# Gates and ups by one 512-column product: high and low half of the operand side by side, and the halves added by VectorE

## The chip, the cores and the metric

One core of a Trainium2 chip runs the whole program. The metric is the device time of one execution in microseconds (us). The kernel before takes 1074.58 us (median of 3 runs, 1074.38 to 1074.78).

## The reference, cut to what matters

Two layers of a context-and-latent block are followed by a second block of two layers (one attention each) whose second half is a convolutional feed-forward network. Only this network is touched by the change. Its width is 2816, the model width 1024, and there are 256 tokens, all in fp32:

```
def conv_ffn(xn, w_gate, conv_w, conv_b, w_up, w_down):
    g = xn @ w_gate
    gp = jnp.pad(g, ((0, 0), (CONV_WIDTH - 1, 0), (0, 0)))
    gc = conv_b + sum(conv_w[j] * gp[:, j:j + S] for j in range(CONV_WIDTH))
    h = jax.nn.gelu(gc, approximate=False) * (xn @ w_up)
    return h @ w_down
h = h + conv_ffn(rms_norm(h, norm_ffn[i]), ...)     # for i in 0, 1
```

## The kernel before

Every fp32 matrix is split into a high part (rounded to the `fp32r` type) and the rest, the low part. A product is then three matmuls in `fp32r`: high weight by high operand, high weight by low operand, low weight by high operand (`products`, lines 435 to 439). The operand's parts are the tiles OPH and OPL, the weight's parts the three buffers `whi` and `wlo`.

Weights arrive as chunks of 1 MB. SP issues one DMA per chunk into one of three `raw` buffers, when the low part of the chunk three before it is made. ACT copies each half of a chunk to `whi` (`split_hi`, line 400), DVE subtracts it to `wlo` (`split_lo`, line 415). A buffer pair is free when the product with the chunk three before it is done. `split_hi(e, n)` stands in the code where ACT is to have split all chunks below number n; so the place of the call sets ACT's order, and `split_lo` does the same for DVE. All engines work in the order of the code.

The network of a layer (`ffn`) goes through its 2816 columns in 11 passes of 256 (two tiles of 128). Pass c has a chunk for the gate, one for the up product and one for the down product. TensorE's order is gate 0 with up 0 (block by block of the operand), the sum of squares of the norm (line 1008), gate 1, up 1, down 0, gate 2, up 2, down 1, and so on; gate c+1 and up c+1 always stand ahead of down c. A gate or an up chunk is two tiles by eight blocks of the operand, 16 products or 48 matmuls of 256 columns. A down chunk is 48 such matmuls in layer 0 (`narrow`) and 24 of 512 columns in layer 1 (`by_token`), which puts 16 transposes ahead of its first chunk.

In a pass, ACT makes the norm's factor (only at the start, `inverse_root`, lines 1015 and 1019); DVE multiplies the gate's bank by it into a padded tile (line 2959); ACT makes the newest tap of the convolution (2927) and DVE adds two more (2965); ACT takes the Gelu (2934); DVE multiplies the up bank by the factor (2977) and by the Gelu (2980); ACT copies the result to its high part (2939) and DVE subtracts that for the low part (2984), the operand of the down product. Gate and up results alternate over four PSUM banks, so each has a second bank while the first is read. The stage ahead of the network, `added`, uses banks 0 and 1 and empties them into X on DVE (line 2592).

Of the kernel before, what the change touches and what calls it, by code (L numbers as in the profile page):

```python
# [24 lines left out]
P = 128  # L25
# [224 lines left out]
def program(nc, known, stream, first, con, gate_b, b_s, w_s, last_gain, out):  # L250

    with ExitStack() as ctx:
# [4 lines left out]
        def sb(name, shape, dt=F32):  # L257
            return ctx.enter_context(nc.sbuf_tensor(name, shape, dt))
# [5 lines left out]
        OPH, OPL = sb("OPH", [P, KD, T], F32R), sb("OPL", [P, KD, T], F32R)  # L264
# [2551 lines left out]
        def ffn(l, wo, op_free, lo, hidden):  # L2816
# [12 lines left out]
            pad = [PROJ[:, 8192 + 516 * i:8192 + 516 * (i + 1)].rearrange("p (a b) -> p a b", b=SEQ + 2)  # L2829
                   for i in range(2)]  # L2830
            g, up, t1, t2 = [], [], [], []
            for c in range(NF):
# [4 lines left out]
                by["gate", c].used, by["up", c].used = g[c].full, up[c].full  # L2837
                by["down", c].used = ("down_added", l, c)

            def two(m):  # L2840
# [1 line left out]

            rr = r.unsqueeze(1).broadcast_to([P, 2, SEQ])

            def wide(e, u, ch):
                for point in due(e, u.empty, ch.lo):
                    e.wait_ge(*point)
                for t in range(2):
                    for k in range(KD):
                        for point in due(e, op_block(k)):  # L2850
                            e.wait_ge(*point)
                        mm = products(u.mem[:, t * SEQ:(t + 1) * SEQ], cols(ch, k, t * P, P), op(k, lo, SEQ), k == 0,
                                      k == KD - 1)
                mm.then_inc(*raises(u.full))
# [39 lines left out]
            def pe(e):  # L2894
                both = [(g[0], by["gate", 0]), (up[0], by["up", 0])]
                for k in range(KD):
                    for u, ch in both:
                        for point in due(e, u.empty, ch.lo[k // 4], op_block(k)):
                            e.wait_ge(*point)
                        for t in range(2):  # L2900
                            mm = products(u.mem[:, t * SEQ:(t + 1) * SEQ], cols(ch, k, t * P, P), op(k, lo, SEQ),
                                          k == 0 and t == 0, k == KD - 1, skip=True)
                        if k == KD - 1:
                            mm.then_inc(*raises(u.full))
                total.add(e)
                for what, c, ch in order[2:]:
                    if what == "gate":
                        wide(e, g[c], ch)
                    elif what == "up":
                        wide(e, up[c], ch)  # L2910
                    elif l == 0:
                        narrow(e, c, ch)
                    else:
                        by_token(e, c, ch)

            def act(e):
                operand.act(e)
                log_exp_table()
                split_hi(e, first.s + 4)
                inverse_root(e, f"ffn{l}", r, total.tot.mem[:, 0:SEQ], 1.0 / D, total.full, total.tot.read["act"])  # L2920
                for c in range(NF):
                    j = 2 * c
                    split_hi(e, by["gate", c].s + (3 if c else 4))
                    for point in due(e, ("gate_scaled", l, c), t1[c].empty):
                        e.wait_ge(*point)
                    for b in range(2):
                        nc.scalar.activation(t1[c].mem[:, b * SEQ:(b + 1) * SEQ],  # L2927
                                                  pad[c % 2][:, b, 2:SEQ + 2], ACT.Identity,
                                                  bias=vec("conv_b", 22 * l + j + b),
                                                  scale=vec("conv_w", 66 * l + 44 + j + b)).then_inc(*raises(("newest_tap", l, c) if b else ("tap_made", l, c)))  # L2930
# [12 lines left out]
                for i in range(1, 4 if l == 0 else 1):  # L2943
                    s.gives.act(e, (2 * i - 2, 2 * i - 1))

            def dve(e):
                operand.dve(e)
# [2 lines left out]
                split_lo(e, first.s + 3)  # L2950
                for c in range(NF):
                    j = 2 * c
                    split_lo(e, by["gate", c].s + (3 if c else 4))
                    for point in due(e, g[c].full, ("factor_made", f"ffn{l}"), ("pads_zeroed", l, c % 2)):
                        e.wait_ge(*point)
                    if c >= 2:
                        for point in due(e, ("newest_tap", l, c - 2), ("conv_done", l, c - 2)):
                            e.wait_ge(*point)
                    nc.vector.tensor_tensor(pad[c % 2][:, :, 2:SEQ + 2], two(g[c].mem), rr, ALU.mult).then_inc(*raises(("gate_scaled", l, c)))  # L2959
                    for point in due(e, ("newest_tap", l, c), ("gate_scaled", l, c)):  # L2960
                        e.wait_ge(*point)
                    for tap in (1, 0):
                        for b in range(2):
                            x = t1[c].mem[:, b * SEQ:(b + 1) * SEQ]
                            ins = nc.vector.scalar_tensor_tensor(x, pad[c % 2][:, b, tap:tap + SEQ],  # L2965
                                                                 vec("conv_w", 66 * l + 22 * tap + j + b), x,
                                                                 ALU.mult, ALU.add)
                            if tap:
                                ins.then_inc(*raises(("older_tap", l, c, b)))
                            else:  # L2970
                                ins.then_inc(*raises(("conv_done", l, c) if b else ("conv_half_done", l, c)))
                        if tap:
                            e.wait_ge(*when(("older_tap", l, c, 1)))
                    split_lo(e, by["up", c].s + 3)
                    for point in due(e, up[c].full, t2[c].empty):
                        e.wait_ge(*point)
                    nc.vector.tensor_tensor(two(t2[c].mem), two(up[c].mem), rr, ALU.mult).then_inc(*raises(up[c].read["dve"]))
                    for point in due(e, ("gelu_made", l, c), up[c].read["dve"]):
# [8 lines left out]
                split_lo(e, by["down", NF - 1].s + 3)  # L2987
                for i, a in enumerate(acc if l == 0 else ()):
                    for point in due(e, given[i]):
                        e.wait_ge(*point)  # L2990
                    x = X[:, 2 * i:2 * i + 2, 0:SEQ]
                    nc.vector.tensor_tensor(x, two(a.mem), x, ALU.add).then_inc(*raises(a.read["dve"]))
                    if i:
                        s.gives.dve(e, (2 * i - 2, 2 * i - 1))

            for c in range(NF):
                g[c].freed[:] = [("gate_scaled", l, c)]
                t1[c].freed[:] = [t2[c].full]
                t2[c].freed[:] = [("h_lo_made", l, c)]

# [5 lines left out]
            s.operand_used = [up[NF - 1].full]  # L3006
            return s


# [806 lines left out]
```

## Time and profile before

| | us |
|---|---|
| median of 3 runs | 1074.58 |
| the profiled execution | 1075.35 |
| its span in the trace | 1072.7 |
| TensorE busy, matmul | 1064.1 (99%) |
| TensorE busy, weight loads | 949.9 (89%) |
| VectorE busy | 721.6 (67%) |
| ScalarE busy | 574.9 (54%) |

In the profile's rows PE is TensorE's matmuls, PEld its weight loads, DVE VectorE, ACT ScalarE, POOL GpSimd. A matmul's duration holds its way through the array, so consecutive matmuls overlap; the distance of their starts tells what one costs. The profile's chain of work that ended last gives 96% of the span to PE, and 76% of it to the three lines of `products`.

### The profile page before, as it was taken

Reading aid. Unit: us, or ns where it says so; the run is one execution under the profiler, and the core shown is the slowest. Engines: PE = TensorE matmul, PEld = TensorE weight load, DVE = VectorE, ACT = ScalarE, POOL = GpSimd, SP = SyncE. Lnnn points to the kernel's source line nnn. Section 1 sums busy time; section 2 is a strip of 40 time slices with the busy share of each in tenths; the row PEclk is TensorE's granted clock in tenths of the full one; section 3 lists DMA queues with packets and bytes.
Section 4 is the critical chain, followed back from the end, with each engine's and each line's share of the span. In section 5 each row is a group of like instructions: output and inputs, shape, how many; then the busy total and the mean of one; then the engine's idle time right before and its main releaser. Section 6 shows DMA issues by size and latency. Waiting matters only on the chain.

```text
span 1072.7 us, 19921 instructions
## 1 busy us (share of the span) xinstructions
PE 1064.1 (99%) x8092; PEld 949.9 (89%) x8092; DVE 721.6 (67%) x1230; ACT 574.9 (54%) x977; POOL 141.2 (13%) x166
## 2 busy tenths in 40 slices
PE   9999999999999999999999999999999999999998
PEld 7887878656898999799999999999998799999997
DVE  5665566387554878778875676666677776766674
ACT  4532676544444567866565554444574555545454
POOL 0000010253200001632531000000023410000000
PEclk9999999999999999999999999999999999999999
DMA  9732121286613442057444364555543334555641
GB/s 382 319 137 66 75 79 40 93 289 213 232 41 119 141 145 80 6 193 236 148 168 158 119 236 161 194 186 170 198 155 103 134 119 153 202 201 177 211 178 39
DMA packets 25386, 168.77 MB, mean 157 GB/s; under 512 B 3280, under 2 KB 3536, under 8 KB 5456
## 3 DMA queue, kind: packets, MB, share of 16 engines
q1 hardware_dynamic: 25152, 167.25, 44.1%
q8 instruction: 64, 1.05, 0.4%
q10 hardware_dynamic: 144, 0.26, 0.1%
q14 instruction: 26, 0.21, 0.1%
HBM read 164.35 MB, written 1.05 MB: 154 GB/s over the span
## 4 chain that ended last, share of the span: by engine, by line
PE 96%; DVE 2%; ACT 2%; issue 0%; DVEq 0%; ACTq 0%
PE bank L437 26%; PE bank L438 25%; PE bank L439 25%; PE bank L1550 2%; PE bank L494 2%; PE bank L1714 2%; PE bank L1704 2%; PE bank L1694 1%; PE bank L1577 1%; PE bank L1568 1%; PE bank L446 1%; PE bank L2363 1%; PE bank L1395 1%; DVE wlo L415 1%; ACT TILE L1753 1%; PE bank L1688 1%
## 5 line engine op out<-in xcount | busy, mean ns | idle before, releaser
L437 PE MATMUL bank<-OPH,whi 128*128 128x256 f32 (+1 forms) x1716 | 519.7, 303 | 0.3
L439 PE MATMUL bank<-OPH,wlo 128*128 128x256 f32 (+1 forms) x1716 | 511.2, 298 | 0.0
L438 PE MATMUL bank<-OPL,whi 128*128 128x256 f32 (+1 forms) x1716 | 511.2, 298 | 0.0
L415 DVE TENSOR_TENSOR wlo<-raw,whi 128x1024 fp32r<-128x1024 f32 (+1 forms) x255 | 304.0, 1234 | 101.4 <-ACT whi L400 101.3
L437 PEld LDWEIGHTS bank<-OPH,whi 128*128 128x128 f32 x1716 | 328.0, 191 | 17.3 <-issue 5.2
L438 PEld LDWEIGHTS bank<-OPL,whi 128*128 128x128 f32 x1716 | 328.2, 191 | 10.0 <-issue 1.2
L439 PEld LDWEIGHTS bank<-OPH,wlo 128*128 128x128 f32 x1716 | 328.0, 191 | 9.8
L400 ACT ACTIVATE whi<-raw 128x1024 fp32r<-128x1024 f32 (+1 forms) x255 | 254.9, 1050 | 74.2 <-PE bank L439 71.9
L437 PE MATMUL bank<-whi,OPH 128*128 128x256 f32 (+2 forms) x272 | 93.8, 345 | 0.2 <-DVE OPL L717 0.2
L438 PE MATMUL bank<-wlo,OPH 128*128 128x256 f32 (+2 forms) x272 | 91.1, 335 | 0.0
L439 PE MATMUL bank<-whi,OPL 128*128 128x256 f32 (+2 forms) x272 | 91.1, 335 | 0.0
L2927 ACT ACTIVATE TILE<-PROJ,FIRST 128x256 f32<-128x256 f32 x44 | 24.1, 594 | 82.7 <-DVE PROJ L2959 82.7
L437 PEld LDWEIGHTS bank<-whi,OPH 128*128 128x128 f32 x272 | 51.5, 189 | 7.4 <-issue 1.8
L1774 POOL TENSOR_TENSOR TILE<-TILE,STAT 128x512 f32<-128x512 f32 (+1 forms) x48 | 43.0, 918 | 112.8 <-DVE STAT L1765 112.8
L2965 DVE SCALAR_TENSOR_TENSOR TILE<-PROJ,FIRST,TILE 128x256 f32<-128x256 f32 x88 | 38.8, 482 | 26.4 <-ACT TILE L2927 25.6
L1243 ACT ACTIVATE PROJ<-bank 128x512 f32<-128x512 f32 x33 | 19.7, 595 | 66.9 <-PE bank L439 66.8
L438 PEld LDWEIGHTS bank<-wlo,OPH 128*128 128x128 f32 x272 | 51.6, 190 | 4.1 <-issue 0.2
L439 PEld LDWEIGHTS bank<-whi,OPL 128*128 128x128 f32 x272 | 51.5, 189 | 3.9
L999 POOL TENSOR_TENSOR TILE<-TILE 128x512 f32<-128x512 f32 x15 | 21.1, 1409 | 254.5 <-ACT TILE L991 253.8
L2939 ACT ACTIVATE OPH<-TILE 128x512 fp32r<-128x512 f32 x22 | 13.9, 632 | 62.2 <-DVE TILE L2980 62.2
L1646 POOL TENSOR_TENSOR TILE<-TILE,STAT 128x128 f32<-128x128 f32 x64 | 36.2, 595 | 68.4 <-DVE STAT L1600 68.4
L1753 ACT ACTIVATE TILE<-bank,STAT 128x512 f32<-128x512 f32 (+1 forms) x48 | 29.1, 611 | 27.0 <-DVE STAT L1742 27.0
(291 smaller groups left out, 1132.6 us busy)
## 6 DMA issues: line engine op xcount, KB each, us to landing
raw<-in_stream SPq DMA_DIRECT2D x143, 1024.0 KB, 4.9
PROJ<-in_stream SPq DMA_DIRECT2D x5, 1024.0 KB, 18.4
raw<-in_stream SPq DMA_DIRECT2D x4, 1056.0 KB, 8.6
PROJ<-PROJ SPq DMA_DIRECT2D x32, 64.0 KB, 3.9
FIRST<-in_first SPq DMA_DIRECT2D x1, 1248.0 KB, 5.9
C<-in_con SPq DMA_DIRECT2D x1, 1157.5 KB, 7.2
FIRST<-in_first SPq DMA_DIRECT2D x1, 1024.0 KB, 8.0
WST<-in_w_s SPq DMA_DIRECT2D x2, 256.0 KB, 7.3
```

What stands on the lines that cost most here:

```text
L400: nc.scalar.activation(c.w[0][:, part], c.raw[:, part], ACT.Copy).then_inc(*raises(c.hi[h]))
L415: nc.vector.tensor_tensor(c.w[1][:, part], c.raw[:, part], c.w[0][:, part].bitcast(F32), ALU.subtract).then_inc(*raises(c.lo[h]))
L437: nc.tensor.matmul(out, w[0], x[0], start=start, stop=False, skip_group_check=skip)
L438: nc.tensor.matmul(out, w[0], x[1], start=False, stop=False, skip_group_check=skip)
L439: return nc.tensor.matmul(out, w[1], x[0], start=False, stop=stop, skip_group_check=skip)
L494: mm = nc.tensor.matmul(row.mem[32 * j:32 * j + 32, 256 * n:256 * (n + 1)], COND[:, 2 * k:2 * k + 32], c.raw[:, k * 256:(k + 1) * 256], st ...
L1550: mm = nc.tensor.matmul(self.S[p][r].mem[:, at:at + n], q[:, b * P:(b + 1) * P], k[:, 0:n], start=i == 0 and b == 0, stop=i == len(pairs_) ...
L1646: nc.gpsimd.tensor_tensor(x, x, STAT[:, p, 1, i:i + 1].broadcast_to([P, n]), ALU.mult).then_inc(*raises(("p_normed", self.name, p, r) if b ...
L1753: nc.scalar.activation(self.E[j][r].mem[:, 0:n], self.S[j][r].mem[:, 0:n], ACT.Exp, bias=STAT[:, j % 8, 0, r:r + 1], accum_out=STAT[:, j % ...
L1774: nc.gpsimd.tensor_tensor(x, x, STAT[:, j % 8, 1, r:r + 1].broadcast_to([P, n]), ALU.mult).then_inc(*raises(("p_normed", self.name, j, r)))
L2927: nc.scalar.activation(t1[c].mem[:, b * SEQ:(b + 1) * SEQ], pad[c % 2][:, b, 2:SEQ + 2], ACT.Identity, bias=vec("conv_b", 22 * l + j + b), ...
L2965: ins = nc.vector.scalar_tensor_tensor(x, pad[c % 2][:, b, tap:tap + SEQ], vec("conv_w", 66 * l + 22 * tap + j + b), x, ALU.mult, ALU.add)
```

## The change

OPH and OPL become the two halves of one tile OPS, side by side for each block. For gates and ups a product is now two matmuls: high weight by both halves of the operand at once (512 columns, a whole bank), then low weight by the high half (256 columns, added to the bank's first half). Each of the two tiles of a chunk so fills a bank of its own: gates always use banks 2 and 3, ups banks 0 and 1. ACT copies the second halves of both banks to a tile `part`, DVE adds the first halves to it, and only then comes the multiplication by the norm's factor, now from SBUF. Banks are free when that addition is done.

```
+        def products_apart(bank, w, k, lo, start, stop):
+            both = bank[:].rearrange("p (a b) -> p a b", b=SEQ)
+            nc.tensor.matmul(both, w[0], OPS[:, k, :, lo:lo + SEQ], start=start, stop=False, skip_group_check=True)
+            return nc.tensor.matmul(bank[:, 0:SEQ], w[1], OPH[:, k, lo:lo + SEQ], start=False, stop=stop,
+                                    skip_group_check=True)
...
-                g.append(GBANK.take("pe", ("dve",)))
-                up.append(GBANK.take("pe", ("dve",)))
+                g.append([b.take("pe", ("dve",)) for b in banks[2:4]])
+                up.append([b.take("pe", ("dve",)) for b in banks[0:2]])
...
+            def copy_halves(e, what, c, us, both):
+                for point in due(e, us[0].full, us[1].full, ("halves_summed", l, c - 1, what) if c else None):
+                    e.wait_ge(*point)
+                nc.scalar.activation(part[what], both[:, :, SEQ:2 * SEQ], ACT.Copy).then_inc(
+                    *raises(("low_copied", l, c, what)))
+
+            def add_halves(e, what, c, out, both):
+                for point in due(e, ("low_copied", l, c, what), t2[0].empty if c == 0 and what == "up" else None):
+                    e.wait_ge(*point)
+                nc.vector.tensor_tensor(out, both[:, :, 0:SEQ], part[what], ALU.add).then_inc(
+                    *raises(("halves_summed", l, c, what)))
...
             def pe(e):
                 both = [(g[0], by["gate", 0]), (up[0], by["up", 0])]
                 for k in range(KD):
-                    for u, ch in both:
-                        for point in due(e, u.empty, ch.lo[k // 4], op_block(k)):
+                    for us, ch in both:
+                        for point in due(e, [u.empty for u in us], ch.lo[k // 4], op_block(k)):
                             e.wait_ge(*point)
...
             def act(e):
                 operand.act(e)
                 log_exp_table()
+                split_hi(e, first.s + 3)
+                copy_halves(e, "gate", 0, g[0], g_both)
+                copy_halves(e, "up", 0, up[0], up_both)
+                inverse_root(e, f"ffn{l}", r, total.tot.mem[:, 0:SEQ], 1.0 / D, total.full, total.tot.read["act"])
                 split_hi(e, first.s + 4)
-                inverse_root(e, f"ffn{l}", r, total.tot.mem[:, 0:SEQ], 1.0 / D, total.full, total.tot.read["act"])
                 for c in range(NF):
                     split_hi(e, by["gate", c].s + (3 if c else 4))
+                    if c:
+                        copy_halves(e, "gate", c, g[c], g_both)
...
                     nc.scalar.activation(t1[c].mem[:], t1[c].mem[:], ACT.Gelu).then_inc(*raises(("gelu_made", l, c)))
+                    if c:
+                        copy_halves(e, "up", c, up[c], up_both)
+                    split_hi(e, by["up", c].s + 4)
...
                     nc.scalar.activation(HH[c % 2], two(t2[c].mem), ACT.Copy).then_inc(*raises(("h_hi_made", l, c)))
-                    split_hi(e, by["up", c].s + 4)
-                log_exp_table()
-                split_hi(e, by["down", NF - 1].s + 3)
+                if l:
+                    log_exp_table()
+                split_hi(e, by["down", NF - 1].s + 2.5)
                 for i in range(1, 4 if l == 0 else 1):
                     s.gives.act(e, (2 * i - 2, 2 * i - 1))
+                    if i == 1:
+                        split_hi(e, by["down", NF - 1].s + 3)
+                log_exp_table()
...
             def dve(e):
...
+                    add_halves(e, "gate", c, padded, g_both)
+                    if c == 0:
+                        add_halves(e, "up", 0, two(t2[0].mem), up_both)
+                        split_lo(e, first.s + 4)
...
-                    nc.vector.tensor_tensor(pad[c % 2][:, :, 2:SEQ + 2], two(g[c].mem), rr, ALU.mult).then_inc(*raises(("gate_scaled", l, c)))
+                    nc.vector.tensor_tensor(padded, padded, rr, ALU.mult).then_inc(*raises(("gate_scaled", l, c)))
...
-                    nc.vector.tensor_tensor(two(t2[c].mem), two(up[c].mem), rr, ALU.mult).then_inc(*raises(up[c].read["dve"]))
+                    if c:
+                        add_halves(e, "up", c, two(t2[c].mem), up_both)
...
+                    nc.vector.tensor_tensor(two(t2[c].mem), two(t2[c].mem), rr, ALU.mult).then_inc(*tick("dve"))
```

The change also writes the first pass of a layer in another order. These are ACT's rows of that pass in layer 0, from the split of the second and third weights to the high part of the down product's operand; `whi<-raw` x2 is the split of one chunk, KDUP the norm's factor. Before:

```order
L400 ACTIVATE whi<-raw 128x1024 x4
L1015 ACTIVATE KDUP<-bank,SINGLES 128x256
L1019 ACTIVATE KDUP<-KDUP 128x256
L2927 ACTIVATE TILE<-PROJ,FIRST 128x256 x2
L2934 ACT_TABLE_LOAD
L2934 ACTIVATE TILE<-TILE 128x512
L2939 ACTIVATE OPH<-TILE 128x2x256
L400 ACTIVATE whi<-raw 128x1024 x2
```

And now, in the same place on ACT:

```order
L401 ACTIVATE whi<-raw 128x1024 x2
L2869 ACTIVATE PROJ<-bank 128x512 x2
L1023 ACTIVATE KDUP<-bank,SINGLES 128x256
L1027 ACTIVATE KDUP<-KDUP 128x256
L401 ACTIVATE whi<-raw 128x1024 x2
L2953 ACTIVATE TILE<-PROJ,FIRST 128x256 x2
L2960 ACT_TABLE_LOAD
L2960 ACTIVATE TILE<-TILE 128x512
L401 ACTIVATE whi<-raw 128x1024 x2
L2968 ACTIVATE OPS<-TILE 128x2x256
```

The two copies and the factor moved ahead of the split of up 1, and the split of down 0 moved ahead of the high part. On DVE the rows of the same pass, from the split of gate 1 to that of down 0, were these:

```order
L415 TENSOR_TENSOR wlo<-raw,whi 128x1024 x4
L2959 TENSOR_TENSOR PROJ<-bank,KDUP 128x2x256
L2965 SCALAR_TENSOR_TENSOR TILE<-PROJ,FIRST,TILE 128x256 x4
L2977 TENSOR_TENSOR TILE<-bank,KDUP 128x512
L2980 TENSOR_TENSOR TILE<-TILE 128x512
L2984 TENSOR_TENSOR OPL<-TILE,OPH 128x2x256
L415 TENSOR_TENSOR wlo<-raw,whi 128x1024 x2
```

And they are now, on DVE:

```order
L416 TENSOR_TENSOR wlo<-raw,whi 128x1024 x2
L2875 TENSOR_TENSOR PROJ<-bank,PROJ 128x2x256
L2875 TENSOR_TENSOR TILE<-bank,PROJ 128x512
L416 TENSOR_TENSOR wlo<-raw,whi 128x1024 x2
L2999 TENSOR_TENSOR PROJ<-PROJ,KDUP 128x2x256
L3005 SCALAR_TENSOR_TENSOR TILE<-PROJ,FIRST,TILE 128x256 x4
L3021 TENSOR_TENSOR TILE<-TILE,KDUP 128x512
L3025 TENSOR_TENSOR TILE<-TILE 128x512
L3029 TENSOR_TENSOR OPS<-TILE,OPS 128x2x256
L416 TENSOR_TENSOR wlo<-raw,whi 128x1024 x2
```

Two additions came in between the split of gate 1 and that of up 1; the rest keeps its order.

## Rows read from the trace of the kernel before

**Rows 1.** The page: span, TensorE's granted clock in 40 slices (tenths)

```profile
span 1072.7 us, 19921 instructions
...
PEclk9999999999999999999999999999999999999999
```

**Rows 2.** PE's timeline in an up chunk: start us, duration us, engine, line, operation

```profile
660.14 0.28 PE L437 MATMUL bank<-OPH,whi 128*128 128x256 f32 x1
...
660.50 0.28 PE L437 MATMUL bank<-OPH,whi 128*128 128x256 f32 x1
```

**Rows 3.** PE's timeline where products have 512 columns

```profile
64.55 0.39 PE L437 MATMUL bank<-OPH,whi 128*128 128x512 f32 x1
...
65.23 0.39 PE L437 MATMUL bank<-OPH,whi 128*128 128x512 f32 x1
```

**Rows 4.** PE's timeline where 400 columns stand ahead of 512

```profile
20.08 0.34 PE L439 MATMUL bank<-whi,OPL 128*128 128x400 f32 x1
20.26 0.39 PE L437 MATMUL bank<-OPH,whi 128*128 128x512 f32 x1
20.49 0.40 PE L438 MATMUL bank<-OPL,whi 128*128 128x512 f32 x1
```

**Rows 5.** Busy time by engine, passes 3 to 10 of layer 0

```profile
640.00:760.00 120.00, 120.00 (x1003) 120.00 (x1002) 80.00 (x98) 56.93 (x70) 0.00 (x0) 1.00 0.53 185
```

**Rows 6.** DVE's timeline: the gate of pass 3, idle time and releaser in brackets

```profile
640.18 0.69 DVE L2959 TENSOR_TENSOR PROJ<-bank,KDUP 128x512 f32<-128x512 f32 x1 [2.13 <-PE bank L439]
```

**Rows 7.** PE's timeline, first pass of layer 0: gate 1 begins, up 1 ends, down 0

```profile
599.01 0.47 PE L437 MATMUL bank<-OPH,whi 128*128 128x256 f32 x1
...
610.60 0.28 PE L439 MATMUL bank<-OPH,wlo 128*128 128x256 f32 x1
611.00 0.36 PE L437 MATMUL bank<-OPH,whi 128*128 128x256 f32 x1
```

**Rows 8.** ACT's timeline, first pass of layer 0

```profile
598.31 2.01 ACT L400 ACTIVATE whi<-raw 128x1024 fp32r<-128x1024 f32 x2 [6.81 <-PE bank L439]
600.22 0.45 ACT L1015 ACTIVATE KDUP<-bank,SINGLES 128x256 f32<-128x256 f32 x1
600.71 0.42 ACT L1019 ACTIVATE KDUP<-KDUP 128x256 f32<-128x256 f32 x1
...
605.45 0.63 ACT L2934 ACTIVATE TILE<-TILE 128x512 f32<-128x512 f32 x1 [0.56 <-DVE TILE L2965]
606.85 0.63 ACT L2939 ACTIVATE OPH<-TILE 128x512 fp32r<-128x512 f32 x1 [0.77 <-DVE TILE L2980]
607.39 1.99 ACT L400 ACTIVATE whi<-raw 128x1024 fp32r<-128x1024 f32 x2
```

**Rows 9.** DVE's timeline, end of the stage before and first pass of layer 0

```profile
587.45 0.69 DVE L2592 TENSOR_TENSOR FIRST<-bank,FIRST 128x512 f32<-128x512 f32 x1 [0.59 <-PE bank L439]
...
599.50 2.36 DVE L415 TENSOR_TENSOR wlo<-raw,whi 128x1024 fp32r<-128x1024 f32 x2 [4.81 <-ACT whi L400]
601.78 0.69 DVE L2959 TENSOR_TENSOR PROJ<-bank,KDUP 128x512 f32<-128x512 f32 x1
603.62 1.80 DVE L2965 SCALAR_TENSOR_TENSOR TILE<-PROJ,FIRST,TILE 128x256 f32<-128x256 f32 x4 [1.16 <-ACT TILE L2927]
...
607.51 0.69 DVE L2984 TENSOR_TENSOR OPL<-TILE,OPH 128x512 fp32r<-128x512 f32 x1 [0.70 <-ACT OPH L2939]
608.53 2.36 DVE L415 TENSOR_TENSOR wlo<-raw,whi 128x1024 fp32r<-128x1024 f32 x2 [0.33 <-ACT whi L400]
```

**Rows 10.** ACT's timeline: a copy of 512 columns out of a bank

```profile
504.56 0.60 ACT L1243 ACTIVATE PROJ<-bank 128x512 f32<-128x512 f32 x1 [1.96 <-PE bank L439]
```

**Rows 11.** The chain that ended last: the transposes ahead of down 0, layer 1

```profile
902.07 1.75 PE bank L2880 x16
```

**Rows 12.** DMA issues: weight chunks, size, median us to landing

```profile
raw<-in_stream SPq DMA_DIRECT2D x143, 1024.0 KB, 4.9
```

**Rows 13.** Who waited for whom, PE: total us, times, longest

```profile
PE bank L446 <- DVE ONES L767: 1.1, 1, 1.1
```

More of the change, by code:

```diff
@@ L2831, in ffn @@
             g, up, t1, t2 = [], [], [], []
+            g_both, up_both = twin[1], twin[0]
+            part = {what: PROJ[:, at:at + 512].rearrange("p (a b) -> p a b", b=SEQ)
+                    for what, at in (("gate", 9224), ("up", 9736))}
             for c in range(NF):
-                g.append(GBANK.take("pe", ("dve",)))
-                up.append(GBANK.take("pe", ("dve",)))
+                g.append([b.take("pe", ("dve",)) for b in banks[2:4]])
+                up.append([b.take("pe", ("dve",)) for b in banks[0:2]])
                 t1.append(tile.take("act", ("dve",)))
                 t2.append(tile.take("dve", ("act", "dve")))
-                by["gate", c].used, by["up", c].used = g[c].full, up[c].full
+                by["gate", c].used, by["up", c].used = g[c][1].full, up[c][1].full
                 by["down", c].used = ("down_added", l, c)
@@ L2843, in ffn, with wide @@
             rr = r.unsqueeze(1).broadcast_to([P, 2, SEQ])
-            def wide(e, u, ch):
-                for point in due(e, u.empty, ch.lo):
+            def wide(e, us, ch):
+                for point in due(e, ch.lo):
                     e.wait_ge(*point)
-                for t in range(2):
+                for t, u in enumerate(us):
+                    for point in due(e, u.empty):
+                        e.wait_ge(*point)
                     for k in range(KD):
[L2850 to L2854, printed above, removed]
+                        mm = products_apart(u.mem, cols(ch, k, t * P, P), k, lo, k == 0, k == KD - 1)
+                    mm.then_inc(*raises(u.full))
+            def copy_halves(e, what, c, us, both):
[5 more added lines that the diff above has]
+                for point in due(e, ("low_copied", l, c, what), t2[0].empty if c == 0 and what == "up" else None):
+                    e.wait_ge(*point)
+                nc.vector.tensor_tensor(out, both[:, :, 0:SEQ], part[what], ALU.add).then_inc(
+                    *raises(("halves_summed", l, c, what)))
             def narrow(e, c, ch):
@@ L2896, in pe @@
                 for k in range(KD):
-                    for u, ch in both:
-                        for point in due(e, u.empty, ch.lo[k // 4], op_block(k)):
+                    for us, ch in both:
+                        for point in due(e, [u.empty for u in us], ch.lo[k // 4], op_block(k)):
                             e.wait_ge(*point)
[L2900 to L2904, printed above, removed]
+                        for t, u in enumerate(us):
+                            mm = products_apart(u.mem, cols(ch, k, t * P, P), k, lo, k == 0, k == KD - 1)
+                            if k == KD - 1:
+                                mm.then_inc(*raises(u.full))
                 total.add(e)
@@ L2952, in dve @@
                     j = 2 * c
-                    split_lo(e, by["gate", c].s + (3 if c else 4))
-                    for point in due(e, g[c].full, ("factor_made", f"ffn{l}"), ("pads_zeroed", l, c % 2)):
+                    padded = pad[c % 2][:, :, 2:SEQ + 2]
+                    if c:
+                        split_lo(e, by["gate", c].s + 3)
+                    for point in due(e, ("pads_zeroed", l, c % 2)):
                         e.wait_ge(*point)
@@ L2958, in dve @@
                             e.wait_ge(*point)
-                    nc.vector.tensor_tensor(pad[c % 2][:, :, 2:SEQ + 2], two(g[c].mem), rr, ALU.mult).then_inc(*raises(("gate_scaled", l, c)))
+                    add_halves(e, "gate", c, padded, g_both)
+                    if c == 0:
+                        add_halves(e, "up", 0, two(t2[0].mem), up_both)
+                        split_lo(e, first.s + 4)
+                    for point in due(e, ("halves_summed", l, c, "gate"), ("factor_made", f"ffn{l}")):
+                        e.wait_ge(*point)
+                    nc.vector.tensor_tensor(padded, padded, rr, ALU.mult).then_inc(*raises(("gate_scaled", l, c)))
                     for point in due(e, ("newest_tap", l, c), ("gate_scaled", l, c)):
@@ L2968, in dve @@
                             if tap:
-                                ins.then_inc(*raises(("older_tap", l, c, b)))
+                                ins.then_inc(*raises(("conv_done", l, c, "older", b)))
                             else:
-                                ins.then_inc(*raises(("conv_done", l, c) if b else ("conv_half_done", l, c)))
+                                ins.then_inc(*raises(("conv_done", l, c) if b else ("conv_done", l, c, "half")))
                         if tap:
-                            e.wait_ge(*when(("older_tap", l, c, 1)))
+                            e.wait_ge(*when(("conv_done", l, c, "older", 1)))
                     split_lo(e, by["up", c].s + 3)
-                    for point in due(e, up[c].full, t2[c].empty):
+                    for point in due(e, t2[c].empty):
                         e.wait_ge(*point)
-                    nc.vector.tensor_tensor(two(t2[c].mem), two(up[c].mem), rr, ALU.mult).then_inc(*raises(up[c].read["dve"]))
-                    for point in due(e, ("gelu_made", l, c), up[c].read["dve"]):
+                    if c:
+                        add_halves(e, "up", c, two(t2[c].mem), up_both)
+                    for point in due(e, ("halves_summed", l, c, "up")):
+                        e.wait_ge(*point)
+                    nc.vector.tensor_tensor(two(t2[c].mem), two(t2[c].mem), rr, ALU.mult).then_inc(*tick("dve"))
+                    e.wait_ge(*ticked("dve"))
+                    for point in due(e, ("gelu_made", l, c)):
                         e.wait_ge(*point)
@@ L2992, in dve @@
                     nc.vector.tensor_tensor(x, two(a.mem), x, ALU.add).then_inc(*raises(a.read["dve"]))
-                    if i:
+                    if i == 0:
+                        split_lo(e, by["down", NF - 1].s + 2.5)
+                    else:
                         s.gives.dve(e, (2 * i - 2, 2 * i - 1))
+                    if i == 1:
+                        split_lo(e, by["down", NF - 1].s + 3)
             for c in range(NF):
-                g[c].freed[:] = [("gate_scaled", l, c)]
+                for i in range(2):
+                    g[c][i].freed[:] = [("halves_summed", l, c, "gate")]
+                    up[c][i].freed[:] = [("halves_summed", l, c, "up")]
                 t1[c].freed[:] = [t2[c].full]
@@ L3005, in ffn @@
             s.used = [("down_added", l, NF - 1)]
-            s.operand_used = [up[NF - 1].full]
+            s.operand_used = [up[NF - 1][1].full]
             return s
```

6 lines of the change are left out of this document (3 added, 3 removed).

## The prediction

> **What bounds the kernel now.** I read the page first, then TensorE's timeline, then the two engines that feed it. The span is 1072.7 us of an execution of 1075.35 us, with the granted clock full in all 40 slices [rows 1]. In passes 3 to 10 of layer 0 TensorE is busy for all of 120 us, DVE for 80 and ACT for 57 [rows 5], and the gate's result is waited for by DVE, 2.13 us each pass, not the other way round [rows 6]. So in the steady passes the matmuls set the time, and only their number and price count there. In the first pass of each layer it is otherwise: there everything hangs on one chain through ACT and DVE. Up 1's last matmul starts at 610.60, so down 0 could start at 610.72; it starts at 611.00 [rows 7], 0.11 after DVE's low part of its weights ends at 610.89 [rows 9].
>
> **What the product saves.** Three matmuls of 256 columns take 0.36 us, 120 ns each [rows 2]. Three of 512 take 0.68, 227 each [rows 3]. After 400 columns the next one starts 180 ns later, and after those 512 columns 230 later [rows 4]. At 2.4 GHz the columns alone are 107, 167 and 213 ns, so each matmul carries some 13 ns more whatever its width, and what it costs hangs on its own columns, not on its neighbour's. The new pair then costs 227 + 120 = 347 ns against 360. There are 2 layers x 11 passes x 32 such products, 704: 9.4 us off, 4.7 a layer. No row has 512 columns read as two runs of 256, nor 512 and 256 in turn. The bounds are 333 ns (the 512 without its surcharge) and 360 (no gain); I take 347, as three widths agree.
>
> The Trainium skill, "TensorE: Matmul & The Clock Gate", section "Back-to-back issue gap", gives an isolated matmul N / 2.4 + 2.5 ns. By it the triple would be 327.5 ns and the pair 325.0, so only 1.8 us would be saved in all; the trace disagrees by some 11 ns a matmul, and the trace decides. That result is a rival below.
>
> **Steady passes.** Each adds two copies on ACT (0.60 each, [rows 10]) and two additions on DVE (0.69 each, like the other operations of this size in [rows 9]). A pass falls from 144 x 0.12 = 17.28 to 16.85 us. DVE's share of [rows 5], 80 of 120, is 11.5 us a pass and becomes 12.9; ACT's 8.2 becomes 9.4. Both stay below 16.85. With one bank pair each for gate and up, TensorE needs the additions done one pass later, 11 us after the products; copy and addition take under 1.5. I cost these at nothing, up to 1 us in all. The weights' DMAs wait for the low part of the chunk three before and land in 4.9 us [rows 12]; even the latest chunk below has over 10 us, so SP's queue changes nothing.
>
> **The first pass of layer 0, step by step.** Zero is where gate 1 begins, 599.01 before [rows 7].
> First, up 0 now needs banks 0 and 1, the latter emptied by DVE only at 587.45 + 0.69 = 588.14 [rows 9]. The joint phase of gate 0 and up 0 is 96 matmuls, 11.52 us, and the sum of squares takes 0.24, so it began at 587.25. Gate's block takes 0.69, then TensorE stands until 588.25, with the restart 0.40.
> Next, before, ACT is let go at -0.70 [rows 8], 0.26 after the last gate matmul. Now four matmuls (0.69) and the sum (0.24) stand between, so the gate's copy starts at -0.67 and the up copy at 0.02. DVE adds from 0.00 and from 0.69. Gate 1 must wait for the first addition, since it has no second bank: 0.80 lost.
> ACT then makes the factor at 0.52 (0.49 and 0.42, [rows 8]) and splits up 1 from 1.36; before it did that from -0.70. DVE has up 1's low part 1.19 + 2.36 us later [rows 8, 9], at 4.91, and scales the gate at 4.83 (601.78 before, which is 2.77). From there the rows of before hold: 1.84 to the taps, 1.83 to the Gelu [rows 8, 9]: 8.50. Then ACT splits down 0 ahead of the high part, 9.04 to 11.03 (1.99, [rows 8]), the high part starts at 10.95 and the low part at 11.61 (0.66 later, as 606.85 to 607.51), and only behind it DVE makes down 0's low part, 12.22 to 14.58. Before, the same two steps ran side by side. Down 0 starts at 14.69; before at 11.99. TensorE, with gate 1 from 0.80, 32 products of 0.347 and 0.19 for the restart after the sum (seen in [rows 7]: 599.01 + 11.52 against 610.72), is free at 12.1. It loses 2.6, where it lost 0.28.
> Then the queue runs on. Down 0 ends at 20.45. DVE, free at 14.50, has to add, scale, make taps and only then split gate 2: 14.50 + 0.80 + 1.84 + 1.72 + 2.36 = 21.2, and 0.87 more is lost. Behind gate 2's split stand the addition, two multiplications (0.79 each with their wait), the high part and the low part, then up 2's split, done at 27.1 where TensorE comes at 26.9: 0.3. From down 1 on it is ahead again.
> Layer 0 loses 0.40 + 0.80 + 2.6 + 0.87 + 0.3 = 5.0, against 0.28 before; the saving is 4.7. Nothing is left: 0.0.
>
> **Layer 1.** The same, except that 1.75 us of transposes stand ahead of down 0's wait [rows 11] and cover as much of the 2.6, leaving 0.85. Down 0 is 24 x 0.227 = 5.44 there, 0.32 less, so gate 2 is waited for 0.32 longer, 1.19. At the end, from the last gate's bank to the low part for down 10 is copy 0.67, addition 0.79, scaling to taps 1.84, taps 1.72, a split 2.28, addition and two multiplications 2.31, high and low part 1.45, with 0.26 release 11.3, while up 10 and down 9 give 5.55 + 5.44: 0.35. Together 0.40 + 0.80 + 0.85 + 1.19 + 0.3 + 0.35 = 3.9 against nothing before: 0.8 gained. In layer 0 down 9 is longer and hides this, and down 10 (5.76 us) covers the splits put between the last additions into X: at nothing, up to 1 us.
>
> **The sum.** The profiled execution goes from 1075.35 by 0.8 to 1074.6. The median of the runs is 0.77 below the profile, so the forecast is 1073.8. A change below 0.2%, 2.1 us, can't be told from none.
>
> **Rivals.** *The queue of the first passes is shorter than laid out* (faster). The schedule adds up 8.9 us of holds from durations and releases; if half of that is not there, because ACT's copies or splits overlap better or a TensorE hold swallows the next, the time is 1073.8 - 4.5 = 1069.3; without any hold 1064.9. For it: every hold is a difference of long sums, and a hold of one pass makes room in the next. Against it: before's own row at 611.00 comes out by the same steps to 0.1 us, and the order of ACT and DVE is fixed. The pair at 340 ns instead of 347 would give the same 4 to 5 us.
> *The clock falls* (slower). In layer 0 TensorE stands for 2.6 us ahead of down 0; before, its longest wait is 1.1 us [rows 13], with full clock throughout [rows 1], so no row shows a pause like this. If the granted clock went to 1.2 GHz, down 0's columns would take twice their time: at most 5.8 us for the whole chunk, 1079.6. It decides from the point where more than some 2.9 us of that is lost; a short fall stays within no change.
> The Trainium skill, same page, section "Why this matters for your kernels", warns of pauses between bursts of matmuls because the clock goes back to its half level; that speaks against this change, and no run here shows it for a pause of this length.
> *The wide product saves nothing* (slower). If the 512-column matmul read in two runs costs as much as two of 256, the pair is 360: the holds shrink by about 1 us, as TensorE comes later, and 7.6 of them stay: 1074.58 + 7.3 = 1081.9. Against it stand the three widths; for it only that no row has this form. The page's 325 against 327.5 lies near this end.
>
> **Chances.** No change, 1071.7 to 1075.9 as the likeliest case's own range: 0.46, and 0.06 more for a short fall of the clock. Shorter queue or cheaper pair: 0.26. A clock that stays low beyond 0.2%: 0.06. Holds longer than laid out by 2 us or more: 0.10; nothing saved: 0.06. That makes faster 0.26, same 0.52, slower 0.22. The range, 1068.8 to 1078.5, reaches half way into the faster case and into the clock's.
>
> **What would show it.** In the profile after: a pass of 16.85 us; 0.347 from one wide product to the next; in layer 0 a TensorE wait of about 2.6 us on down 0's low part near 611 to 614, one of 0.8 on the addition ahead of gate 1, 0.9 ahead of gate 2, 0.4 near 588. Wrong if a pass stays at 17.28, if the wait ahead of down 0 is under 1.5, or if the granted clock in the slice behind it is below full.

## The result, and the profile after

The changed kernel takes 1077.55 us (median of 8 runs, 1076.39 to 1080.35) against 1074.74 for the kernel before on the same chip (1074.38 to 1075.62): a ratio of 1.0026, 95% interval 1.0018 to 1.0035. It is 2.8 us slower, a change that can be told from none. The forecast was 1073.8 and no change; the time lies inside the range. The profiled execution is one of the quicker ones of the eight, at 1076.87 us.

The page after, against [rows 1]: the span is longer by 2.3 us, the granted clock nine tenths or more in every slice of this execution.

```profile
span 1075.0 us, 18604 instructions
...
PEclk9999999999999999999999999999999999999999
```

Where the 2.3 us arise can be read from three matmuls on TensorE's timeline that stand in both kernels and don't belong to the stage: one ahead of layer 0's feed-forward stage, the first sum of squares behind it, and the last matmul of all. First the kernel before, then the one after (start us, duration us, engine, line, operation).

```profile
570.16 0.44 PE L1577 MATMUL bank<-TILE,PROJ 128*64 128x256 f32 x2
...
789.75 0.38 PE L1008 MATMUL bank<-TILE,ONES 128*128 128x256 f32 x1
...
1067.15 0.39 PE L439 MATMUL bank<-whi,OPL 128*128 128x512 f32 x1
```

```profile
569.95 0.44 PE L1585 MATMUL bank<-TILE,PROJ 128*64 128x256 f32 x2
...
791.24 0.38 PE L1016 MATMUL bank<-TILE,ONES 128*128 128x256 f32 x1
...
1069.36 0.39 PE L440 MATMUL bank<-whi,OPS 128*128 128x512 f32 x1
```

From the first to the second it is 219.59 before and 221.29 after: layer 0 loses 1.70 us. From the second to the third, 277.40 and 278.12: layer 1 loses 0.72. The forecast was 0.0 and a gain of 0.8.

The waits of TensorE that are new, after (who waited for whom, us in total, times, longest), where before the longest was 1.1 [rows 13]:

```profile
PE bank L438 <- DVE wlo L416: 3.1, 2, 2.4
PE bank L445 <- DVE wlo L416: 1.4, 2, 0.8
...
PE bank L445 <- DVE PROJ L2875: 1.0, 2, 0.5
```

Each line is two waits, one a layer: down 0 and gate 2 for their weights' low part, gate 1 for the first addition. On TensorE's timeline of layer 0 they look like this (compare the one short stop of [rows 7]):

```profile
587.63 0.28 PE L446 MATMUL bank<-OPS,wlo 128*128 128x256 f32 x1
587.99 0.51 PE L445 MATMUL bank<-OPS,whi 128*128 128x512 f32 x1
...
598.70 0.59 PE L1016 MATMUL bank<-TILE,ONES 128*128 128x256 f32 x2
599.79 0.47 PE L445 MATMUL bank<-OPS,whi 128*128 128x512 f32 x1 [0.49 <-DVE PROJ L2875]
...
610.85 0.28 PE L446 MATMUL bank<-OPS,wlo 128*128 128x256 f32 x1
613.55 0.36 PE L438 MATMUL bank<-OPS,whi 128*128 128x256 f32 x1 [2.42 <-DVE wlo L416]
...
619.25 0.28 PE L440 MATMUL bank<-OPS,wlo 128*128 128x256 f32 x1
620.11 0.47 PE L445 MATMUL bank<-OPS,whi 128*128 128x512 f32 x1 [0.58 <-DVE wlo L416]
```

From one start to the next, less what that matmul takes when nothing holds it: 0.25 and a restart of 0.10 (the matmul behind the stop comes late too) in the joint phase, 0.85 ahead of gate 1, 2.58 ahead of down 0, 0.74 ahead of gate 2. The idle time in brackets is shorter, since it counts only from the modelled end of the last matmul.

The steady pass is read from DVE's addition for the gate, in two passes that follow each other:

```profile
643.91 0.69 DVE L2875 TENSOR_TENSOR PROJ<-bank,PROJ 128x512 f32<-128x512 f32 x1 [1.37 <-ACT PROJ L2869]
...
660.98 0.69 DVE L2875 TENSOR_TENSOR PROJ<-bank,PROJ 128x512 f32<-128x512 f32 x1 [2.43 <-ACT PROJ L2869]
```

17.07 us, not 16.85. DVE still waits there, as in [rows 6], now for ACT's copy, and TensorE is busy all the time (busy us by engine, PE first, then PEld, DVE, ACT and POOL; granted clock, DMA share, GB/s):

```profile
640.00:760.00 120.00, 120.00 (x789) 109.48 (x788) 90.04 (x115) 64.70 (x84) 0.00 (x0) 1.00 0.52 186
```

So the matmuls cost more than forecast. Call a wide product of 512 columns and its narrow one of 256 a pair, and the distance from one wide product to the next its beat. There are two beats (two stretches of TensorE's timeline after, wide products only):

```profile
602.30 0.39 PE L445 MATMUL bank<-OPS,whi 128*128 128x512 f32 x1
...
603.34 0.39 PE L445 MATMUL bank<-OPS,whi 128*128 128x512 f32 x1
...
640.49 0.39 PE L445 MATMUL bank<-OPS,whi 128*128 128x512 f32 x1
...
641.55 0.40 PE L445 MATMUL bank<-OPS,whi 128*128 128x512 f32 x1
```

Three pairs take 1.04 us at 602 and 1.06 at 640; over eights of pairs it is 346.7 and 353.3 ns. Only some 110 of the 704 pairs run at the faster beat: gate 1 and up 1 of layer 0, and in layer 1 gate 0 with up 0, gate 1, up 1 and up 2.

### The profile page after: what moved, and what is told of

Same layout as the page of the kernel before. It is cut to its first block, busy times and chain, and to the rows that moved or that the text cites. A ratio compares the mean times of both kernels' runs of the same rounds, so it can differ in the third digit from the quotient of the medians.

```text
span 1075.0 us, 18604 instructions
## 1 busy us (share of the span) xinstructions
PE 1060.7 (99%) x7388; PEld 911.6 (85%) x7388; DVE 748.0 (70%) x1274; ACT 598.7 (56%) x1021; POOL 142.0 (13%) x166
## 4 chain that ended last, share of the span: by engine, by line
PE 92%; DVE 4%; ACT 3%; DMA 1%; issue 1%; DVEq 0%; SPq 0%; ACTq 0%
PE bank L438 18%; PE bank L440 17%; PE bank L439 17%; PE bank L445 14%; PE bank L446 7%; PE bank L1558 2%; PE bank L502 2%; PE bank L1722 2%; PE bank L1712 2%; DVE wlo L416 2%; PE bank L1702 1%; PE bank L1585 1%; PE bank L1576 1%; PE bank L2371 1%; DMA FIRST<-in_first 1%; PE bank L1403 1%
## 5 line engine op out<-in xcount | busy, mean ns | idle before, releaser
L438 PE MATMUL bank<-OPS,whi 128*128 128x256 f32 (+1 forms) x1012 | 320.8, 317 | 2.6 <-DVE wlo L416 2.4
L440 PE MATMUL bank<-OPS,wlo 128*128 128x256 f32 (+1 forms) x1012 | 312.6, 309 | 0.0
L439 PE MATMUL bank<-OPS,whi 128*128 128x256 f32 (+1 forms) x1012 | 312.6, 309 | 0.0
L445 PE MATMUL bank<-OPS,whi 128*128 128x512 f32 x704 | 249.6, 399 | 2.6 <-DVE wlo L416 1.4
L438 PEld LDWEIGHTS bank<-OPS,whi 128*128 128x128 f32 x1012 | 193.1, 191 | 19.7 <-issue 5.6
L440 PEld LDWEIGHTS bank<-OPS,wlo 128*128 128x128 f32 x1012 | 193.1, 191 | 9.8
L439 PEld LDWEIGHTS bank<-OPS,whi 128*128 128x128 f32 x1012 | 193.3, 191 | 9.5 <-issue 1.2
L446 PE MATMUL bank<-OPS,wlo 128*128 128x256 f32 x704 | 197.9, 281 | 0.0
L445 PEld LDWEIGHTS bank<-OPS,whi 128*128 128x128 f32 x704 | 132.5, 188 | 36.1 <-DVE wlo L416 2.0
L446 PEld LDWEIGHTS bank<-OPS,wlo 128*128 128x128 f32 x704 | 133.3, 189 | 0.3
L438 PE MATMUL bank<-whi,OPS 128*128 128x256 f32 (+2 forms) x272 | 94.2, 346 | 0.8 <-DVE wlo L416 0.7
L440 PE MATMUL bank<-whi,OPS 128*128 128x256 f32 (+2 forms) x272 | 91.4, 336 | 0.0
L439 PE MATMUL bank<-wlo,OPS 128*128 128x256 f32 (+2 forms) x272 | 91.2, 335 | 0.0
L438 PEld LDWEIGHTS bank<-whi,OPS 128*128 128x128 f32 x272 | 51.5, 189 | 8.9 <-issue 2.1
L439 PEld LDWEIGHTS bank<-wlo,OPS 128*128 128x128 f32 x272 | 51.6, 190 | 4.2 <-issue 0.2
```

What stands on the lines that cost most here:

```text
L445: nc.tensor.matmul(both, w[0], OPS[:, k, :, lo:lo + SEQ], start=start, stop=False, skip_group_check=True)
L446: return nc.tensor.matmul(bank[:, 0:SEQ], w[1], OPH[:, k, lo:lo + SEQ], start=False, stop=stop, skip_group_check=True)
```

## The experiments

**The pair by itself** (e1_streams): the program is replaced by streams of matmuls.

```
triples: w_hi x x_hi, w_hi x x_lo, w_lo x x_hi, 256 columns each
pairs:   w_hi x [x_hi | x_lo] read in two runs, w_lo x x_hi
joined:  the same, [x_hi | x_lo] read in one run
grouped: 8 wide, then 8 narrow          turns: two banks by turns
last:    pairs beside 20 splits on ACT and 16 on DVE
```

> Only streams of matrix products, none of the model's computation is left: threes of 256 columns as before the change, then pairs of 512 and 256 columns as after it, with the 512 columns read as two runs or as one, the wide products alone, all wide ones of a bank ahead of its narrow ones, two banks by turns, and at the end threes, pairs and threes beside a busy ScalarE and VectorE. Threes 360 ns throughout. Theory A (the read of two runs costs the missing 6.5 ns): pairs 353 in two runs, 347 in one run, wide alone 233 against 227. Theory B (changing between the two widths costs it): both kinds of pair 353, wide alone 227, grouped 347. Theory C (the other engines cost it): every quiet pair 347, the pairs beside ScalarE and VectorE 353.

Timeline of TensorE: quiet pairs in two runs; joined; pairs beside ACT and DVE (ACT splits from 277.55 to 299.39, DVE to 297.67), wide products only; and the grouped stream (there a row is a whole run of eight).

```profile
104.86 0.40 PE L288 MATMUL bank<-OPS,whi 128*128 128x512 f32 x1
...
105.92 0.40 PE L288 MATMUL bank<-OPS,whi 128*128 128x512 f32 x1
...
121.14 0.40 PE L293 MATMUL bank<-NEXT,whi 128*128 128x512 f32 x1
...
122.20 0.40 PE L293 MATMUL bank<-NEXT,whi 128*128 128x512 f32 x1
...
284.77 0.40 PE L288 MATMUL bank<-OPS,whi 128*128 128x512 f32 x1
...
285.83 0.40 PE L288 MATMUL bank<-OPS,whi 128*128 128x512 f32 x1
...
173.26 2.00 PE L336 MATMUL bank<-OPS,whi 128*128 128x512 f32 x8
...
176.05 2.00 PE L336 MATMUL bank<-OPS,whi 128*128 128x512 f32 x8
```

All three kinds give 1.06 us for three pairs, 353.3 ns, and so do two banks by turns; triples stay at 360, and wide products alone come every 227 ns, in two runs as in one, once the first few are past. So neither the two runs nor the other engines cost it: theories A and C fall. Grouped, eight pairs take 2.79 us, 349 each, near the 347 of theory B. The streams had no stretch at 347, so why the model has some stayed open.

**Grouped in the model** (e2_grouped), each bank's eight wide products ahead of its eight narrow ones, from the second pass on:

```diff
-                    for k in range(KD):
-                        mm = products_apart(u.mem, cols(ch, k, t * P, P), k, lo, k == 0, k == KD - 1)
+                        nc.tensor.matmul(both, cols(ch, k, t * P, P)[0], OPS[:, k, :, lo:lo + SEQ], ...
+                    for k in range(KD):
+                        mm = nc.tensor.matmul(u.mem[:, 0:SEQ], cols(ch, k, t * P, P)[1], OPH[:, k, lo:lo + SEQ], ...
```

> From the second pass on, each bank gets its eight wide products first and its eight narrow ones behind them. Theory B (changing widths costs 6.5 ns a pair): 640 pairs at 347 instead of 353.5, 4.2 us less, about 1073.4, a pass of 16.85. Theories A and C: the pass stays at 17.07 and the time at 1077.5.

1074.57 us, ratio to before 0.9998 (0.9989 to 1.0007): 3.0 us less than the change, and even with the kernel before. In the change some 560 of these 640 pairs ran at 353.3 and 80 at 346.7; at 349 for all of them 2.2 us go. Where the other 0.8 went was not followed.

**When a pair begins** (e5_starts): ahead of each of 17 streams of 24 pairs one matmul of 128, 130, ... 160 columns.

> Again only streams of products. Seventeen times eight threes, then one product of 128 to 160 columns (two more each time, which shifts what follows by 0.8 ns a time), then 24 pairs; behind them two wide and two narrow products by turns, and sixteen wide ahead of sixteen narrow. Theory D (the pair keeps a faster or slower beat by the instant at which it begins): some of the shifts give 347 ns a pair, the others 353, in an order that repeats. Rival: all seventeen give 353, and what made some stretches of the model run at 347 is something else. By theory B the changes of width are what costs: 350 a pair by two and two, under 348 by sixteen.

The first two streams, with 128 and 130 columns:

```profile
69.09 0.22 PE L382 MATMUL bank<-OPS,whi 128*128 128x128 f32 x1
...
69.56 0.40 PE L288 MATMUL bank<-OPS,whi 128*128 128x512 f32 x1
...
77.33 0.40 PE L288 MATMUL bank<-OPS,whi 128*128 128x512 f32 x1
...
80.56 0.22 PE L382 MATMUL bank<-OPS,whi 128*128 128x130 f32 x1
...
81.02 0.40 PE L288 MATMUL bank<-OPS,whi 128*128 128x512 f32 x1
...
88.64 0.40 PE L288 MATMUL bank<-OPS,whi 128*128 128x512 f32 x1
```

From the second pair to the 24th, 7.77 us and 7.62: 353 and 346 ns, and the beat once taken is kept. Of the 17 streams those with 128, 134, 140, 144, 148, 152, 156 and 160 columns run at 353, the other nine at 346 to 347. By two and two the pair is 348.4, by sixteen 347.9.

**The same in the model** (e9_nudged): one matmul of 128 + 2 (c mod 4) columns ahead of each gate from the third pass on.

> The whole change, with one more product of 128, 130, 132 or 134 columns (by the pass) ahead of each gate from the third pass on, its result overwritten by the gate's first product. Theory D (the starting instant sets the beat): some of the 18 passes run their gate and up at 347 instead of 353 ns a pair, by the number of columns, which is worth 0.21 us in such a pass, and each product costs about 0.07 us: a time between 1076.5 and 1078.8. Rival (the beat of 353 belongs to the place in the model): every pass from the third on stays at 353 and the time rises by 1.2 us to 1078.8.

Wide products of passes 5 (130 columns) and 6 (132) of layer 0:

```profile
672.32 0.23 PE L2864 MATMUL bank<-OPS,whi 128*128 128x130 f32 x1
...
672.79 0.40 PE L445 MATMUL bank<-OPS,whi 128*128 128x512 f32 x1
...
683.39 0.40 PE L445 MATMUL bank<-OPS,whi 128*128 128x512 f32 x1
...
689.50 0.23 PE L2864 MATMUL bank<-OPS,whi 128*128 128x132 f32 x1
...
689.97 0.39 PE L445 MATMUL bank<-OPS,whi 128*128 128x512 f32 x1
...
700.37 0.39 PE L445 MATMUL bank<-OPS,whi 128*128 128x512 f32 x1
```

Thirty pairs take 10.60 us in the one and 10.40 in the other. In layer 0 all three passes with 132 columns are fast and the six with other widths slow; in layer 1, whose down has 512 columns, passes 2, 3 and 7 are fast. The time is 1078.17, ratio 1.0031 (1.0019 to 1.0043), inside what theory D allowed, but only 0.6 us from its rival; the passes decide, not the time. The same 132 columns give the fast beat in layer 0 and the slow one in two passes of layer 1, so it isn't the width ahead as such: the instant at which the pairs begin sets the beat.

**DVE's queue ahead of down 0** (e3_low_ahead):

```diff
                     nc.vector.tensor_tensor(t2[c].mem[:], t1[c].mem[:], t2[c].mem[:], ALU.mult)...
+                    if c == 0:
+                        split_lo(e, by["up", c].s + 4)
                     e.wait_ge(*when(("h_hi_made", l, c)))
```

> In the first pass of each feed-forward stage VectorE makes the low part of down 0's weights ahead of the low part of the hidden operand. If the 2.58 us hold ahead of down 0 is the queue of VectorE as the prediction said, it falls to about 1.2 (the low part is then made as soon as ScalarE's half is there) and the run takes 1.0 to 1.6 us less, about 1076.2. Rival: the hidden operand's low part or gate 2's weights come later by as much, and the time stays within 0.3 us of 1077.5.

1073.92, ratio 0.9990 (0.9982 to 0.9999): 3.6 us less than the change, more than expected. DVE's timeline in layer 0, first of the change, then of this version:

```profile
610.49 0.69 DVE L3029 TENSOR_TENSOR OPS<-TILE,OPS 128x512 fp32r<-128x512 f32 x1 [1.65 <-ACT OPS L2968]
611.10 2.36 DVE L416 TENSOR_TENSOR wlo<-raw,whi 128x1024 fp32r<-128x1024 f32 x2
```

```profile
609.23 2.36 DVE L416 TENSOR_TENSOR wlo<-raw,whi 128x1024 fp32r<-128x1024 f32 x2 [0.29 <-ACT whi L401]
611.51 0.68 DVE L3031 TENSOR_TENSOR OPS<-TILE,OPS 128x512 fp32r<-128x512 f32 x1
```

The 1.65 us in which DVE stood are filled, and down 0 starts at 612.45. TensorE's waits of the change fall from 5.5 us in both layers to 3.0: down 0 1.2 (in layer 1 none is left, which the expectation had not counted) and gate 2 0.8. And some 155 pairs, 45 more, run at the faster beat, 0.3 us. Together 2.8, by which the span of the profiled execution is shorter. The other 0.8 of the medians probably goes with the clock (under the rivals below).

**The early copies and additions undone** (e8_first_undone): in the first pass they stand where later passes have them.

```diff
-                split_hi(e, first.s + 3)
-                copy_halves(e, "gate", 0, g[0], g_both)
-                copy_halves(e, "up", 0, up[0], up_both)
+                split_hi(e, first.s + 4)
                 inverse_root(...)
-                split_hi(e, first.s + 4)
...
-                    if c == 0:
-                        add_halves(e, "up", 0, two(t2[0].mem), up_both)
-                        split_lo(e, first.s + 4)
```

> The change without its second half: in the first pass the halves are copied and added where later passes do it, behind the norm's root, the splits and the activation. Then gate 1 waits for gate 0's sum behind two more splits, and up 1 for up 0's sum behind the taps: holds of 1.5 to 4 us more a layer and a time of 1080 to 1085. Rival (the early copies only reorder a queue that is as long either way): within 1 us of 1077.5.

1079.58, ratio 1.0048 (1.0035 to 1.0062), a little less than the 1080 to 1085 expected. TensorE's largest wait here:

```profile
PE bank L445 <- DVE PROJ L2875: 6.5, 2, 3.3
```

Gate 1 now waits 3.3 us in each layer, and the waits ahead of down 0 and gate 2 don't come. The early additions are worth 2.0 us by the medians (part of it may be the clock, which falls behind the longer pause, as the rivals below show), but they spread the wait over three places rather than end it.

**Wide products from the third pass on** (e4_from_third), threes before:

```diff
+            W0 = 2
+                g.append([b.take("pe", ("dve",)) for b in (banks[2:4] if c >= W0 else [banks[2], banks[0]][c:c + 1])])
-                    if c:
+                    if c >= W0:
                         copy_halves(e, "gate", c, g[c], g_both)
```

> The first two passes of each layer as before the change (threes into one bank, no halves to add), the wide products from the third pass on. If the holds of the first pass are what they seem (5.0 and 3.9 us, all gone here) and the pair is worth 6.5 ns: 576 pairs save 3.7 us of the time before, about 1071.0. If the pair is worth 13.3 ns: 1067.1. If the holds are only moved into the third pass, or the saving is lost behind it: 1074 to 1075.

1071.28, ratio 0.9966 (0.9954 to 0.9979), as the pair at 353.3 wants it. The holds are gone but for 0.7 us ahead of down 0, and don't come back in the third pass.

**Both mended** (e7_both_mended): e3's line, and sixteen wide ahead of sixteen narrow.

> The whole change, with sixteen wide ahead of sixteen narrow, and the low part of down 0's weights ahead of the hidden operand's. If the pair and the queue of the first pass are two separate losses, their gains add (3.0 for eight and eight, about 0.7 more for sixteen, and 3.6 for the queue): about 1070.3. If both act on the same holds: 1072.5 or more.

1070.81, ratio 0.9964 (0.9952 to 0.9977): the two gains add to within 0.5 us.

**From the third pass on, by sixteen** (e6_third_grouped): e4 with the grouping, and ACT's copy of the hidden operand ahead of down's weights in the first two passes.

> The wide products from the third pass on, now sixteen wide ones ahead of sixteen narrow ones, and in the first two passes ScalarE's copy of the hidden operand ahead of down's weights, as before the change. Theory B: 576 pairs at 348 instead of 353.3 take 3.1 us from the 1071.28 of the version from the third pass on, and the hold of 0.73 us ahead of down 0 goes back to 0.3: about 1067.8. Rival: the first bank is now full 1.9 us later, ScalarE's copies and VectorE's additions come late and new holds take it back: 1070 to 1071.

1067.46, ratio 0.9934 (0.9921 to 0.9946): the best version, 7.1 us under the kernel before. TensorE in layer 0, an up chunk, the start of a down, and the next up (a row of the products is a run of sixteen):

```profile
655.89 3.82 PE L2875 MATMUL bank<-OPS,whi 128*128 128x512 f32 x16
...
661.46 0.28 PE L438 MATMUL bank<-OPS,whi 128*128 128x256 f32 x1
...
672.78 3.82 PE L2875 MATMUL bank<-OPS,whi 128*128 128x512 f32 x16
```

Sixteen pairs take 5.57 us, 348 each, and from up to up a pass is 16.89.

## Why the prediction was wrong

*The step that failed* is the price of the pair: "what it costs hangs on its own columns, not on its neighbour's ... I take 347". The model pays 353.3 in some 594 of 704 pairs. By 360 - 353.3 for all and 6.6 more for 110, the saving is 704 x 6.7 ns + 110 x 6.6 ns = 5.4 us, not 9.4. [Rows 3] show widths that don't change and [rows 4] a single change, on a timeline in steps of 10 ns; neither is 512 and 256 in turn. The price lay inside the bounds of 333 and 360, but the middle was taken from rows of another kind. e1 shows that each width alone keeps the price forecast (227 and 120 ns); by turns e5 and e9 show either their sum, 346.7, or 6.6 ns more, by the instant at which the pairs begin. Nearly everywhere the model got the dearer one.

*The holds* were right in place and nearly in size. In layer 0: joint phase 0.40 forecast, 0.35 measured; gate 1 0.80 and 0.85; down 0 2.6 and 2.58; gate 2 0.87 and 0.74; up 2 0.3 and under 0.1. Worked back from the lags (1.70 + 0.72) and the saving of 5.4, both layers lose 7.9 against the 8.6 forecast, each beyond what the kernel before lost. So of the 3.2 us between forecast and trace, from -0.8 to +2.4, the pair accounts for 4.0, and holds shorter by 0.7 go the other way. That the time stayed inside the range is partly luck: the two errors have opposite signs. e3 and e8 confirm the chain that was laid out: the wait ahead of down 0 is DVE's queue.

*Steady passes* hide copies and additions, as costed: no wait is left there.

*The rivals.* A shorter queue came in part, 0.7 us of 8.6. The clock is another matter. In the profiled execution of the change it stays full behind the pause ahead of down 0. But in the traces of e2 and e9, which have the same pause (TensorE idle for 2.36 and 2.44 us, against 2.42), and in that of e8, where gate 1 waits 3.25 us in layer 1, it falls to 0.50, the level of 1.2 GHz, right behind the pause. The columns are those of the row above; the change first, then e2, e9 and e8, with the starts of down 0 and gate 2 in e2 at the end:

```profile
614.00:617.00 3.00, 3.00 (x28) 3.00 (x27) 1.76 (x5) 2.19 (x4) 0.00 (x0) 1.00 0.81 257
...
614.00:617.00 3.00, 3.00 (x16) 3.00 (x16) 1.80 (x5) 2.51 (x4) 0.00 (x0) 0.50 0.94 311
...
614.00:617.00 3.00, 3.00 (x15) 3.00 (x15) 1.77 (x5) 2.05 (x4) 0.00 (x0) 0.50 0.77 238
...
895.00:898.00 3.00, 2.84 (x9) 2.49 (x10) 1.77 (x5) 2.20 (x3) 0.00 (x0) 0.50 0.82 268
...
613.23 0.36 PE L438 MATMUL bank<-OPS,whi 128*128 128x256 f32 x1 [2.36 <-DVE wlo L416]
...
620.53 2.00 PE L2864 MATMUL bank<-OPS,whi 128*128 128x512 f32 x8
```

From down 0 to gate 2 it is 7.30 us in e2 against 6.56 in the change's trace (613.55 to 620.11): the fall costs 0.74, because the wait for gate 2's weights disappears in it. Of the change only one execution has a trace, but every run has its span and mean granted clock: two have 0.999 and spans of 1074.5 and 1075.0 us, five have 0.997 or 0.998, as e2 and e9 have, and spans of 1075.6 to 1075.9. The median span, 1075.7, is 0.7 above the trace. The runs of e9 part in the same way, 0.999 with 1076.2 to 1076.3 us and 0.997 or 0.998 with 1076.4 to 1077.2. So the clock probably fell in most executions, and 0.7 of the 2.8 us is its share; that is read from means and not shown by a trace. (The eighth, 1080.35 us with a mean of 0.947, stays unexplained.) In e3, where no such pause is longer than 1.2 us, all eleven runs have 0.999 or 1.000. The prediction gave a short fall of the clock a chance of 0.06 and bounded its price by 5.8 us.

The Trainium skill, "TensorE: Matmul & The Clock Gate", section "Why this matters for your kernels", warns of pauses between bursts. The traces of e2, e8 and e9 agree with it (0.50 behind the pause); that of the change's profiled execution shows no fall (1.00).

"The wide product saves nothing" was too dark, but it named the right doubt: 4.0 of the 9.4 us of saving are gone.

*Left open:* what in the chip makes the beat of 353.3 or 346.7. Shown is that the starting instant sets it and that it then lasts for the whole run of pairs (24 in e5); what the instant meets was not tried. Open too is why the clock fell behind the pause in some executions and not in the profiled one of the change.

## What to carry to other kernels

Price a new order of matmuls from rows in that order: widths by turns can cost more than each width alone, and grouping like widths gave most of it back here without new holds. A saving per pass is earned in the steady passes and lost in the first, where every added copy stands in the chain to the next weights; leave the first passes as they are and change the later ones. Where an engine stands still waiting for another, look for work behind that wait that somebody else needs first. And read the mean granted clock of every run, not only of the profiled one: a pause can lower it in some executions and not in others.

## What the runs showed of the hardware

A matmul of 512 columns and one of 256 by turns take 346.7 or 353.3 ns for the same instructions, 6.6 ns apart, and two columns more in one matmul ahead (128 to 130 in e5) can change one into the other for all 24 pairs that follow. Reading the 512 columns in two runs costs nothing (353.3 either way by turns, 227 either way alone), nor do ACT and DVE beside it. A pause of TensorE of some 2.4 us was followed by a granted clock of 0.50 in two traces (e2, e9) and of 1.00 in a third (the change), at the same place.
